# Scores of the selected and sliding branches from high and low parts, in three passes, two heads side by side

## The reference, cut to what matters

```python
s_c = jnp.einsum('bgrqd,bgnd->bgrqn', qg, kc) * scale          # compressed: 31 keys
...
s_s = jnp.einsum('bgrqd,bgqnld->bgrqnl', qg, k_sel)...* scale  # selected blocks
p_s = masked_softmax(s_s, m_s)...
...
s_w = jnp.einsum('bgrqd,bgkd->bgrqk', qg, k_win) * scale       # sliding window
p_w = masked_softmax(s_w, m_w)
...
o = gc[..., 0:1] * o_c + gc[..., 1:2] * o_s + gc[..., 2:3] * o_w
```

## Time and profile before

| | |
|---|---|
| median of 3 runs | 1712.34 us (1712.15 to 1712.43) |
| the profiled execution, its own time | 1712.49 us |
| span of its trace | 1710.7 us |
| PE busy | 1685.8 us, 99% of the span |
| POOL, ACT, DVE busy | 819.2, 712.5, 652.3 us |

### The profile page before, as it was taken

One profiled execution on the slowest core, in us unless ns is written; L12 is line 12 of the kernel. 1 busy time (PEld: TensorE's weight loads), 2 busy tenths in 40 slices (PEclk: granted clock), 3 DMA queues, 4 the chain that ended last, 5 costly groups with the idle time before them and its releaser, 6 DMA issues.

```text
span 1710.7 us, 22973 instructions
## 1 busy us (share of the span) xinstructions
PE 1685.8 (99%) x9123; PEld 1364.2 (80%) x9123; DVE 652.3 (38%) x1413; ACT 712.5 (42%) x1367; POOL 819.2 (48%) x518
## 2 busy tenths in 40 slices
PE   8999999999999999999999999999999999999998
PEld 7888766887788888888878887768877888888886
DVE  3454675152263223311243456652431622232113
ACT  5425777262362222232353367764433612222322
POOL 4356668363134444455624467663632334443552
PEclk9999999999999999999999999999999999999999
DMA  6224112242122333232332340112421233222221
GB/s 204 94 91 137 50 26 51 74 149 99 37 75 99 99 98 99 74 111 90 122 99 84 105 138 26 26 51 87 160 74 51 86 98 99 91 96 84 99 98 74
DMA packets 101189, 154.13 MB, mean 90 GB/s; under 512 B 4396, under 2 KB 76380, under 8 KB 101084
## 3 DMA queue, kind: packets, MB, share of 16 engines
q1 hardware_dynamic: 97790, 147.09, 26.4%
q10 hardware_dynamic: 3294, 5.59, 1.0%
HBM read 150.56 MB, written 2.10 MB: 89 GB/s over the span
## 4 chain that ended last, share of the span: by engine, by line
PE 92%; ACT 3%; DVE 2%; DMA 1%; issue 1%; POOL 1%; DVEq 0%; SPq 0%; ACTq 0%
PE banks L1615 25%; PE banks L1617 25%; PE banks L1616 25%; PE banks L1885 4%; PE banks L1914 4%; PE banks L1938 4%; PE banks L2076 1%; PE banks L2058 1%; PE banks L1717 1%; ACT rows L855 1%; POOL w_lo L764 1%; PE banks L1645 1%; DVE banks L1267 1%; DVE h L1268 1%; PE banks L1934 0%
## 5 line engine op out<-in xcount | busy, mean ns | idle before, releaser
L764 POOL TENSOR_TENSOR w_lo<-raw,w_hi 128x1024 fp32r<-128x1024 f32 (+2 forms) x262 | 628.9, 2420 | 766.9 <-ACT w_hi L893 754.2
L893 ACT ACTIVATE w_hi<-raw 128x1024 fp32r<-128x1024 f32 (+2 forms) x264 | 259.5, 1027 | 728.1 <-PE banks L1617 713.2
L1615 PE MATMUL banks<-w_hi,a_lo 128*128 128x512 f32 (+1 forms) x864 | 332.6, 385 | 0.1
L1616 PE MATMUL banks<-w_lo,a_hi 128*128 128x512 f32 (+1 forms) x864 | 330.1, 382 | 0.0
L1617 PE MATMUL banks<-w_hi,a_hi 128*128 128x512 f32 (+1 forms) x864 | 330.0, 382 | 0.0
L1615 PE MATMUL banks<-a_hi,w_lo 128*128 128x512 f32 x768 | 299.5, 390 | 0.0
L1617 PE MATMUL banks<-a_hi,w_hi 128*128 128x512 f32 x768 | 298.8, 389 | 0.0
L1616 PE MATMUL banks<-a_lo,w_hi 128*128 128x512 f32 x768 | 298.8, 389 | 0.0
L1615 PEld LDWEIGHTS banks<-w_hi,a_lo 128*128 128x128 f32 x864 | 162.2, 188 | 33.3 <-issue 2.2
L1617 PEld LDWEIGHTS banks<-w_hi,a_hi 128*128 128x128 f32 x864 | 162.2, 188 | 31.4
L1616 PEld LDWEIGHTS banks<-w_lo,a_hi 128*128 128x128 f32 x864 | 162.3, 188 | 31.1 <-issue 0.5
(11 more groups left out here) (257 smaller groups left out, 2347.2 us busy)
## 6 DMA issues: line engine op xcount, KB each, us to landing
raw<-in_ffn_w_up SPq DMA_DIRECT2D x44, 1024.0 KB, 5.1
raw<-in_ffn_w_down SPq DMA_DIRECT2D x20, 1024.0 KB, 4.9
raw<-in_w_in SPq DMA_DIRECT2D x19, 1024.0 KB, 5.1
raw<-in_x_wk SPq DMA_DIRECT2D x8, 1024.0 KB, 5.3
raw<-in_x_wv SPq DMA_DIRECT2D x8, 1024.0 KB, 4.9
raw<-in_x_wq SPq DMA_DIRECT2D x8, 1024.0 KB, 5.1
raw<-in_x_wo SPq DMA_DIRECT2D x8, 1024.0 KB, 4.9
raw<-in_cmp_wk SPq DMA_DIRECT2D x4, 1024.0 KB, 5.4
```

The lines of the kernel that those rows point to most:

```text
L764: inc(pool.tensor_tensor(lo_half(u, half), raw_half(u, half), hi_half(u, half).bitcast(F32), ALU.subtract), lo_made, n)
L893: inc(act.activation(hi_half(u, half), raw_half(u, half), ACT.Copy), hi_made)
L1615: pe.matmul(dst, st_lo, mv_hi, start=first, stop=False)
L1616: pe.matmul(dst, st_hi, mv_lo, start=False, stop=False)
```

## The change

Queries of the NSA pairs and the keys of both branches (the 32 compressed ones too) are kept as a high part in fp32r and a low part. `scores` of sel and win items issues three fp32r matmuls for each head, with the two heads alternating inside each pass, in place of one float32 matmul for each head. The six head blocks that hold those queries and keys (j = 6, 7, 8, 9, 12, 13) are each read twice: ACT writes the high part, then DVE, after a wait for it, writes the value minus the high part. Blocks 0, 2, 4 and 10 stay with ACT and 1, 3, 5 and 11 with DVE. The scores of moba and sb items stay as they are.

```diff
+def split(j):
+    kind, row = BLOCKS[j]
+    return 2 <= row < 6 if kind == "q" else row >= 4
+def on_act(j):
+    return j % 2 == 0 and not split(j)
...
-        nsa_kT = view("nsa_kT", [P, CMPP + 2 * S], F32, X + (KD + 4) * S * 4)
+        q_hi = view("q_hi", [P, 8, S], F32R, X)
+        nsa_k_hi = view("nsa_k_hi", [P, CMPP + 2 * S], F32R, X + (KD + 4) * S * 4)
+        nsa_k_lo = new("nsa_k_lo", [P, CMPP + 2 * S], F32R)
...
+        q_lo = view("q_lo", [P, KD, S], F32R, R)
...
                 def block_copy(j):
                     act.wait_ge(blk_psum.sem, blk_psum.at(l, 8 + j + 1))
+                    if split(j):
+                        hi, _, scale = split_dst(j)
+                        inc(act.activation(hi, bank(block_bank(j)), ACT.Copy, scale=scale), blk_hi)
+                        return
...
-                        if j % 2 == 0:
+                        if split(j) or on_act(j):
                             block_copy(j)
...
                 def block_copy(j):
+                    if split(j):
+                        hi, lo, scale = split_dst(j)
+                        dve.wait_ge(blk_hi.sem, blk_hi.at(l, blocks_split(j + 1)))
+                        inc(dve.scalar_tensor_tensor(lo, bank(block_bank(j)), scale, hi.bitcast(F32), ALU.mult, ALU.subtract), blk_dve)
+                        return
...
-                            dve.memset(nsa_kT[:, NCMP:CMPP], 0.0)
-                            inc(dve.tensor_copy(nsa_kT[:, 0:NCMP], bank(7, NCMP, 384)), kcT_ready)
+                            dve.memset(nsa_k_hi[:, NCMP:CMPP].bitcast(F32), 0.0)
+                            dve.memset(nsa_k_lo[:, NCMP:CMPP].bitcast(F32), 0.0)
+                            link(dve.tensor_copy(nsa_k_hi[:, 0:NCMP], bank(7, NCMP, 384)))
+                            inc(dve.tensor_tensor(nsa_k_lo[:, 0:NCMP], bank(7, NCMP, 384), nsa_k_hi[:, 0:NCMP].bitcast(F32), ALU.subtract), kcT_ready)
...
-                        if j % 2:
+                        if not on_act(j):
                             block_copy(j)
...
+                        if on_act(j - 3):
+                            pe.wait_ge(blk_act.sem, blk_act.at(l, blocks_on_act(j - 2)))
+                        else:
+                            pe.wait_ge(blk_dve.sem, blk_dve.at(l, j - 2 - blocks_on_act(j - 2)))
...
-                    for hp in range(2):
-                        half = slice(HD * hp, HD * hp + HD)
-                        ins = pe.matmul(s_bank(i, hp, n + extra, key_at(i) - extra), qT[half, m, P * t:P * t + P], keys(row, n, extra)[half],
-                                        start=True, stop=True)
+                    halves = [slice(HD * hp, HD * hp + HD) for hp in range(2)]
+                    tokens = slice(P * t, P * t + P)
+                    if kind in ("moba", "sb"):
...
+                    else:
+                        k_hi, k_lo = (nsa_keys(v, kind, n, extra) for v in (nsa_k_hi, nsa_k_lo))
+                        for p, (q, k) in enumerate(((q_lo, k_hi), (q_hi, k_lo), (q_hi, k_hi))):
+                            for hp, half in enumerate(halves):
+                                ins = pe.matmul(s_bank(i, hp, n + extra, key_at(i) - extra), q[half, m, tokens], k[half], start=p == 0, stop=p == 2)
                     if key_at(i) > CMPP:
...
+                        for p, (q, k) in enumerate(((q_lo, nsa_k_hi), (q_hi, nsa_k_lo), (q_hi, nsa_k_hi))):
+                            for hp, half in enumerate(halves):
+                                ins = pe.matmul(s_bank(i, hp, CMPP), q[half, m, tokens], k[half, 0:CMPP], start=p == 0, stop=p == 2)
```

More of the change, by code:

```diff
@@ L168, in in_part, with blocks_on_act, blocks_split @@
     return divmod(u, 2) if u < 8 else (4 + (u - 8) // 4, (u - 8) // 2 % 2)
+def split(j):
[3 more added lines that the diff above has]
+    return j % 2 == 0 and not split(j)
+def blocks_on_act(n):
+    return sum(on_act(j) for j in range(n))
+def blocks_split(n):
+    return sum(split(j) for j in range(n))
 def block_bank(j):
@@ L261, in build @@
         oT = view("oT", [P, KD, S], F32, R)
+        q_lo = view("q_lo", [P, KD, S], F32R, R)
         rope_tmp = view("rope_tmp", [P, 4, T * 64], F32, R)
         twice = view("twice", [P, T, 4, 2, HD], F32, R + 4096)
-        w2 = view("w2", [P, 2, 2, HD], F32, R + 11904)
-        cg = view("cg", [P, 2, 256], F32, R + 12928)
+        w2 = view("w2", [P, 2, 2, HD], F32, R + 12288)
+        cg = view("cg", [P, 2, 256], F32, R + 13312)
         cgT = view("cgT", [P, 2, 2, T, CMPP], F32, R + 8192)
@@ L377, in build @@
         blk_psum = signal("blk_psum", 22)
-        blk_act = signal("blk_act", 7)
-        blk_dve = signal("blk_dve", 7)
+        blk_act = signal("blk_act", blocks_on_act(len(BLOCKS)))
+        blk_hi = signal("blk_hi", blocks_split(len(BLOCKS)))
+        blk_dve = signal("blk_dve", len(BLOCKS) - blocks_on_act(len(BLOCKS)))
         xb_added = signal("xb_added", 1)
@@ L607, in s_bank, with nsa_keys @@
             return bank(2 * (scored(i) % 2) + hp, n, at)
[L609 to L614, removed]
+        def nsa_keys(v, kind, n, extra=0):
+            at = CMPP + S * (kind == "win")
+            return v[:, at - extra:at + n]
         def cmp_scores(m):
@@ L685, in block_dst, with split_dst @@
             kind, row = BLOCKS[j]
-            return (qT[:, row, :], HD ** -0.5) if kind == "q" else (keys(row, S), 1.0)
+            return (qT[:, row, :], HD ** -0.5) if kind == "q" else (kT[:, row, :], 1.0)
+        def split_dst(j):
+            kind, row = BLOCKS[j]
+            if kind == "q":
+                return q_hi[:, row, :], q_lo[:, row, :], HD ** -0.5
+            row = ("sel", "win")[row - 4]
+            return nsa_keys(nsa_k_hi, row, S), nsa_keys(nsa_k_lo, row, S), 1.0
         def down_parts(k, n=1):
@@ L1724, in head_block @@
                     if j >= 5:
-                        done = blk_act if (j - 3) % 2 == 0 else blk_dve
-                        pe.wait_ge(done.sem, done.at(l, (j - 3) // 2 + 1))
+                        if on_act(j - 3):
+                            pe.wait_ge(blk_act.sem, blk_act.at(l, blocks_on_act(j - 2)))
+                        else:
+                            pe.wait_ge(blk_dve.sem, blk_dve.at(l, j - 2 - blocks_on_act(j - 2)))
                     block_transpose(block_bank(j), lambda t: proj[:, t, col:col + P])
@@ L1880, in scores @@
                         pe.wait_ge(kcT_ready.sem, kcT_ready.at(l, 1))
-                    row = {"moba": m, "sel": 4, "win": 5, "sb": m - 4}[kind]
                     extra = CMPP if beside(i) else 0
-                    for hp in range(2):
-                        half = slice(HD * hp, HD * hp + HD)
-                        ins = pe.matmul(s_bank(i, hp, n + extra, key_at(i) - extra), qT[half, m, P * t:P * t + P], keys(row, n, extra)[half],
-                                        start=True, stop=True)
+                    halves = [slice(HD * hp, HD * hp + HD) for hp in range(2)]
+                    tokens = slice(P * t, P * t + P)
+                    if kind in ("moba", "sb"):
+                        for hp, half in enumerate(halves):
+                            ins = pe.matmul(s_bank(i, hp, n), qT[half, m, tokens], kT[half, m if kind == "moba" else m - 4, 0:n], start=True, stop=True)
+                    else:
[3 more added lines that the diff above has]
+                                ins = pe.matmul(s_bank(i, hp, n + extra, key_at(i) - extra), q[half, m, tokens], k[half], start=p == 0, stop=p == 2)
                     if key_at(i) > CMPP:
-                        for hp in range(2):
-                            half = slice(HD * hp, HD * hp + HD)
-                            ins = pe.matmul(s_bank(i, hp, CMPP), qT[half, m, P * t + P:P * t + 2 * P], nsa_kT[half, 0:CMPP], start=True, stop=True)
+                        tokens = slice(P * t + P, P * t + 2 * P)
+                        for p, (q, k) in enumerate(((q_lo, nsa_k_hi), (q_hi, nsa_k_lo), (q_hi, nsa_k_hi))):
+                            for hp, half in enumerate(halves):
+                                ins = pe.matmul(s_bank(i, hp, CMPP), q[half, m, tokens], k[half, 0:CMPP], start=p == 0, stop=p == 2)
                     inc(ins, qk)
@@ L1898, in transposes @@
                     if i == 0:
-                        pe.wait_ge(blk_act.sem, blk_act.at(l, 7))
-                        pe.wait_ge(blk_dve.sem, blk_dve.at(l, 6))
+                        pe.wait_ge(blk_act.sem, blk_act.at(l, blocks_on_act(len(BLOCKS))))
+                        pe.wait_ge(blk_dve.sem, blk_dve.at(l, len(BLOCKS) - blocks_on_act(len(BLOCKS)) - 1))
                     if i >= 1:
@@ L1921, in values @@
                     if i == 0:
-                        pe.wait_ge(blk_dve.sem, blk_dve.at(l, 7))
+                        pe.wait_ge(blk_dve.sem, blk_dve.at(l, len(BLOCKS) - blocks_on_act(len(BLOCKS))))
                     pe.wait_ge(copied_act.sem, copied_act.at(l, i + 1))
```

## The result

The changed kernel takes 1715.67 us (median of 15 runs, 1713.78 to 1716.76) against 1712.31 (15 runs, 1711.74 to 1712.73): +3.4 us, a ratio of 1.002 (95% interval 1.0012 to 1.0028). That is on the line between "no change" and "slower" as the prediction draws it, and 1.2 us above its 1714.5. The profiled execution took 1715.1 us, its span is 1713.4, 2.7 more than before.

A forecast was written before the change was run, and what follows sets the result against it. PE's list of instructions was taken as the time. Scores -5.0 and evictions +7.2 gave +2.2 on the span of 1710.7; from the median of 1712.34, forecast 1714.5 us. Range 1708.5 to 1722.5, the forecast's own 1711.1 to 1716.4.

The forecast's parts named there:

- Part 1: Scores of sel and win items on PE: three fp32r passes replace float32, saving 5.0 us in all.
- lower bound, -7.6: Scores' largest saving, in us, if narrow passes need not last the 109 ns of a weight load.
- The narrow rival: Scores items: fp32r passes under 256 columns run at the float32 rate, 7.1 us more, 1721.6 us; chance 0.22.
- Turns: Scores items: a pair's heads take turns at the quick rate, +28 us on the forecast, 1742.5 us; chance 0.06.
- Part 2: Evictions at steps 0 to 3 of the mixer's pipeline: ACT and DVE lack room, 3.6 us a layer, +7.2 us.
- Step 1: Pipeline start: DVE waits 1.15 us for ACT's high part of j = 6, which stands behind the cast of weights.
- Step 2: Pipeline start: DVE's two low parts take 1.42 us, reciprocal and compressed keys some 0.7 instead of 0.19, delaying cgT.
- Steps 3 to 5: Pipeline start: PE waits for cgT, DVE's list through vc_tiles ends late, PE's first filler slips 3.1 us.
- Step 6: After the first filler: DVE's remaining evictions delay its copy of the first transposed probabilities, +0.5 us for PE.
- The hidden start: Evictions at steps 0 to 3 cost PE nothing, leaving only the scores' saving: 1707.3 us; chance 0.08.
- Part 3: Everything else: nsa_k_lo has its own place, no DMA is added, PE's other work is the same; no cost.
- The clock: PE's gap at the first filler might lower its granted clock behind it; named as a failure condition, unpriced.

The follow-up runs named there:

- run 2: The change with nsa_k_lo allocated behind all other buffers: 1712.67 us against 1712.29 for the kernel before.
- run 4: New scores alone: three fp32r passes on high parts only, evictions as before, added buffer last and unused: 1707.28 us against 1712.29 before.
- run 8: The change, added buffer last, but steps 0 to 3 evict once in float32 and steps 4 to 8 split from SBUF: 1707.04 us against 1712.14 before.
- run 6: The change with nsa_k_lo last and all three passes of one head issued before the other's: 1713.25 us against 1712.14 before.
- run 3: New evictions alone: the change with nsa_k_lo last, scores back to float32 matmuls on the high parts: 1717.62 us against 1712.29 before.
- run 5: The change, nsa_k_lo in its place, with 14 unread transposes filling PE's gap before the scores of item 4: 1714.62 us against 1712.14 before.
- run 7: The change with nsa_k_lo last and ACT's step 0 cast of weights moved behind step 1: 1711.12 us against 1712.14 before.
- run 1: The kernel before plus an unused buffer of 4224 bytes per partition where the change has nsa_k_lo: 1713.74 us against 1712.29.
- run 9: The kernel before plus an unused buffer of 4096 bytes per partition at nsa_k_lo's place: 1712.08 us against 1712.07.
- run 10: The kernel before plus an unused buffer of 128 bytes per partition at nsa_k_lo's place: 1713.98 us, ratio 1.0011.
- run 11: On run 8, sb scores also in three passes, with four more high and low parts split: 1708.93 us against 1712.07 for the kernel before.

## Why the prediction was right, and where it was not

**Part 1, the scores: right.** Start to start the items take 889 to 897 ns at 512 columns (predicted 875), about 725 at 384 (715), 552 to 556 at 256 (556), 480 at 128 (480), 592 at 288 (595), 495 to 498 at 160 (494), and 995 to 1004 for the two scores in one (998). A pair of heads saves 309 ns in its win and 283 in its sel items (predicted 333 and 295), 8 x 0.592 = 4.7 us; some 0.5 us of it turns into waits, among them two items of 128 columns that hold PE for 0.65 us. The sum is 4.2 us (2.1 in each layer of runs 2, 4 and 8) in place of 5.0, between the bounds. In the lower bound, -7.6, one term is wrong: by the prediction's own formula a pass of 160 columns without the 109 ns saves 29 ns, so an item 59 and not 84, which makes it -7.5.

**The narrow rival is refuted** by the item of 128 columns at 480 ns, where it wanted 849: its passes start 0.11 us apart, one load of weights. 32 columns more, in the items of 160, add 15 to 18 ns, where the slow rate would add 160. **Turns is refuted** by the 0.90 us at 512 columns, where it wanted above 1.5, and again by run 6. For the heads side by side the prediction had only the Trainium skill ("TensorE: Matmul & The Clock Gate", Measured speedup vs the span model); the trace agrees with it as far as two tiles go, with 0.23 us from pass to pass for both heads.

**Part 2, the evictions: the mechanism right, the size not.** 4.6 us in place of 7.2. Measured from the first scores of the layer, so that the offset of the two executions falls out:

- Step 1, DVE's wait for the first high part: 1.17 us, predicted 1.15.
- Step 2, low parts at 0.71 each: mis-sized. They follow each other in 160.33 - 159.12 = 1.21 us for two, 0.61 each. The price came from a row whose scale is an operand; the change's is a constant, and it lasts 0.69 where that one lasts 0.75. With the two of step 4 that is 0.4 us a layer.
- Step 2, the compressed keys at 0.7: mis-sized. From the reciprocal to `cgT` it is 160.75 - 160.33 = 0.42 us; the two clearings of a column run under the copy of the high part (160.43 and 160.44 against 160.42). 0.3 us.
- Steps 3 to 5, PE's wait for `cgT` and DVE's list up to `vc_tiles`: in the order predicted, with the row maxima 0.1 us shorter. 3.1 less 0.4, 0.3 and 0.1 is the 2.3 measured.
- Step 6, +0.5 us for the copy of the first transposed probabilities: it did not come. That copy ends at 169.97, 2.48 us behind the first filler and not 2.95 (DVE's two low parts last 1.28 us together), PE starts its next transposes at 169.94, and no wait of PE for `probT` stands in this stretch.

Outside the steps, PE's wait for `a_lo` is 0.5 us longer in every run that has these evictions (the change and runs 2, 3, 5, 6 and 7: 6.0 to 6.1 us) and in none of the others (5.6 or 5.7). The prediction does not have it, and no run shows where it comes from.

**The hidden start is refuted** by run 3, whose loss is 5.3 us, and by the window of 13.58 us.

**Part 3, "PE's other work is the same": wrong.** This is the step that failed. The sum looked at what the allocation of `nsa_k_lo` takes and not at what it moves: the stationary operands behind it leave their alignment, 384 matmuls of 512 columns take 5 ns more, and 384 of 256 columns about 1 ns. Runs 1, 9 and 10 show it alone, 1.5 and 1.9 us in the medians; run 2 takes it away.

**The clock.** The prediction named it as what would make it wrong, and put it at nothing in the sum. The gap of 1.85 us lowered the granted clock in layer 1 of the profiled execution (0.55 over 3.76 us), 1.5 us of loss, and not in layer 0. Over all runs it is worth about 1 us (run 5). The runs themselves bear this out, since the mean granted clock of each is on record: it is 0.997 in the nine from 1715.64 to 1716.76 us, and 0.998 or 0.999 in the six from 1713.78 to 1715.10. A profiled execution with one fall (the change, in layer 1) has 0.998, the one with two (run 6, at the beginning and in layer 1) has 0.997; the kernel before never has less than 0.998 in the 78 runs listed beside the experiments. (The profiled executions also end with 1 to 4 us at the lower level, when PE has no more work, which takes about 0.001 more at most.) So the slower runs of the change have two falls or more. Which of them stand in a mixer only a trace could tell.

Together: -4.2 + 4.6 = +0.4 (run 2: +0.4), 1.5 to 1.9 of addresses, about 1 of clock, 2.9 to 3.3 against +3.4 measured. That the forecast came within 1.2 us is luck: it had 2.6 too much for part 2 and 0.8 too much for part 1's gain, and nothing for the 3 us of addresses and clock.

**Open.** Run 2 has the same gap as the change, yet none of its eleven runs has 0.997 (all have 0.998), where the change has it in nine of fifteen. The one that was profiled has its single fall at the beginning; whether the upper group of six has one in a mixer is not known. The profiled execution of run 6, with the gap too, has the fall at 1017. The Trainium skill ("TensorE: Matmul & The Clock Gate", Part 1: The HAM clock gate) says that the hardware judges PE's activity in windows that do not start with the kernel, so that one kernel can differ from run to run. The runs agree in that the falls come in some executions of a kernel and not in others; none shows why run 2 has fewer of them than the change. The wait for `xv` in layer 0 is absent from the traces of the change and of runs 2, 5, 6, 7, 8 and 11 and is there in those of before and of runs 1, 3, 4, 9 and 10 (0.3 to 1.1 us). ACT's cast ahead of it waits 4.0 to 4.6 us for the DMA `raw<-in_x_wq` where PE waits, and 2.7 to 3.0 us where it does not. No run isolates this, so differences of under 1 us between kernels are not explained here to the last tenth. Nor is it shown why 128 bytes cost a stationary operand 5 ns.

## What to carry to other kernels

Where PE's list is the time, a cheaper form of its operands pays only if the engines that make the form have room at that place: the same split cost 4.6 us in the pipeline's start and nothing four steps later (run 8 keeps the whole 4.2 us of the items). An added buffer is a change of every address behind it: put it last, or compare the groups of untouched matmuls by their mean duration. And a wait that is added just before dense matmuls is priced with what the clock may do behind it, not with its length alone.

## What the hardware did that was not expected

- **Alignment of the stationary operand.** fp32r matmuls of 512 columns go from 227 to 232 ns start to start when the buffer of their stationary operand moves by 128 bytes, and not when it moves by 4096. A streamed operand that moves by 128 bytes costs nothing.
- **A clock fall that only some executions have.** Seven of thirteen profiled executions have a granted clock of 0.79 from 8 to 16 us, whatever the kernel, and are 0.4 to 1.0 us later behind it than the six that have 1.00 there.
- **Heads overlap in either order of issue.** 0.90 us for six passes of 512 columns in two row tiles, whether the passes alternate between the tiles or not (run 6).
- **A low part of 2.90 us.** In both layers of run 8 one low part lasts four times as long as the others, and POOL's subtraction beside it 2.83 in place of 2.37. From DVE's timeline and then POOL's:

```profile
169.14 0.67 DVE L1572 TENSOR_TENSOR q_lo<-qT,q_hi 128x512 fp32r<-128x512 f32 x1
169.73 2.90 DVE L1572 TENSOR_TENSOR nsa_k_lo<-nsa_kT,nsa_k_hi 128x544 fp32r<-128x544 f32 x1
```

```profile
169.22 2.83 POOL L808 TENSOR_TENSOR w_lo<-raw,w_hi 128x1024 fp32r<-128x1024 f32 x1
```

POOL starts inside DVE's first low part and runs 0.46 us long; DVE's second starts inside POOL's and ends 0.58 us behind it. The two take turns by whole instructions. The Trainium skill ("SBUF — State Buffer", SBUF: two separate sides) has this as a lock, for DVE operations with both inputs in SBUF against POOL's reads; the trace agrees. In the change six of the twelve low parts run beside POOL's subtraction and all twelve last 0.68 to 0.69 us; one of their two inputs is in PSUM.
